# Attention heads of the second block in pairs on the two halves of TensorE's columns

## The chip, the cores and the metric

The kernel runs on one core of a Trainium2 chip. The metric is the device time of one execution in microseconds (us); of three runs the median was 3005.82 us. All data are 32-bit floats unless said otherwise.

## The reference

The reference is two transformer blocks on one sequence of 512 tokens and width 1024. The first block (a gated delta rule, a sliding-window attention and a mixture of 32 experts) is not touched. The second block adds a context of 256 tokens and has two layers. Only its attention matters here:

```
layer 1, latent heads (8) and grouped-query heads (8, two heads of keys and values):
    o  = softmax(q k^T * scale) v      for 512 queries over 768 keys (512 tokens + 256 context)
    oc = softmax(qc kc^T * scale) vc   for 256 context queries over the 256 context keys
    mix = concat(o of all heads) * silu(gate);   x = x + gate' * (mix @ w_out)
layer 2, windowed heads (8, two heads of keys and values):
    512 queries in blocks of 128, each over its own block, the one before, the one after (masked)
    and the 256 context keys, with a sink term per head in the softmax's sum
```

A head's values are 64 wide, its queries and keys 64 (grouped-query, windowed) or 96 (latent).

## The kernel before

Four stretches do this attention with the same three functions, one per engine (`pe_attention`, `dve_attention`, `act_attention`, lines 2268 to 2404): the grouped-query heads (`gqa`, 48 units), the latent heads 0 to 3 (`mla0`, 24), the latent heads 4 to 7 (`mla1`, 24) and, in the next layer, the windowed heads (`win`, 32). All engines meet (`meet()`) after each stretch.

A unit is one tile of 128 queries of one head. In layer 1 a head is two groups: one of four main units (768 keys) and one of two late units (the context's queries, 256 keys). In layer 2 a head is one group of four units of 512 or 640 keys. A unit goes through these steps:

- `score` (TensorE, line 2280): the query tile against the keys, into one of two PSUM buffers.
- `soften` (VectorE, line 2333 and after): the row maximum and its negative; in `win` masks are added before it (line 2324).
- `exponentials` (ScalarE, line 2381): the exponential with the row sum.
- `scale` (VectorE, lines 2349 and 2351): the reciprocal of the sum, and the row scaled by it.
- `turn_probs` (TensorE, line 222): each 128x128 tile of probabilities is transposed into a third PSUM buffer; `copy_probs` (ScalarE, line 2391) copies them to `PTM` (main), `PTC` (late) or `PTW` (windowed).
- `values` (TensorE, line 2299), once per group: for each of six key tiles (two for a late group), values (128 keys x 64) as the stationary operand, turned probabilities (128 keys x up to 512 queries) as the moving one, accumulated in PSUM bank 6 on partitions 0 to 63 for even heads, 64 to 127 for odd ones. Each such product shows as two records in the trace. VectorE then multiplies the 64 x 512 (or 64 x 256) result into the gate (line 2358).

The order on TensorE is written out: in iteration x come the scores of unit x+1, then the value products due (`A.sums[x]`), then the turning of unit x-1. `Heads` plans the due ones: when a group's last unit is x-1, its products are queued in iteration x, and from the next iteration on two are done in each. VectorE does maximum, scaling, and then the group's multiplication, in the iteration in which the group's last product is due, and waits there for it. `copy_probs` of a group waits until the values of the group two before are done.

In `gqa` and `mla0` further work for the latent heads (projections, norms, rotations, turnings) is advanced by a generator (`steps(filler, rate)`) twice (gqa) or four times (mla0) in each iteration on every engine.

Weights come through a ring. In the second block load n (2 MB or less) goes to slot n mod 3 and is issued by SP's queue, in order, when the load before it in its slot has been used. Loads 6 and 7 are the two halves of the output projection `w_out` of layer 1 (lines 1284 to 1296: the first half for all six row tiles, then the second), load 8 the first of layer 2. The arrays QT, KT, PTM and PTC lie in `spare`, behind the three slots.

## Time and profile before

| | us |
|---|---|
| median of three runs | 3005.82 (3004.95 to 3008.05) |
| the profiled execution | 3011.71 |
| its span | 3010.5 |
| TensorE busy | 2664.7 (89% of the span) |
| VectorE busy | 1008.3 (33%) |
| ScalarE busy | 565.4 (19%) |
| mean granted TensorE clock | 0.932 of 2.4 GHz |

The four stretches of attention lie at 2117.3 to 2548.6 us of the span (one after the other: gqa, mla0, mla1) and at 2834.5 to 2951.2 us (win). Busy time is the time in which an engine had at least one instruction running; the idle time of an engine that is not the one waited for costs nothing. "PEclk" is the granted clock as a share of 2.4 GHz: 0.50 is 1.2 GHz.

### The profile page before, as it was taken

What the parts mean: (1) busy time and instruction counts of PE and PEld (TensorE: products, weight loads), DVE (VectorE), ACT (ScalarE), POOL (GpSimd) and SP (SyncE); (2) the same over time, 40 slices, a digit from 0 to 9 for tenths busy, and PEclk for the clock granted to TensorE, in tenths of its full rate; (3) what the DMA queues carried; (4) which work ended last, traced back from release to release, by engine and by line L of the source; (5) the groups of instructions that cost most, each with busy time, mean ns of one, the idle gap of its engine ahead of it and who ended that gap; (6) DMA issues with size and microseconds to landing.
All of it is one profiled execution on the core that took longest, in us unless ns stands there. A gap on an engine that the chain in (4) does not pass through costs nothing. (4 is left out here: it accounts for less than half of the span.)

```text
span 3010.5 us, 27117 instructions
## 1 busy us (share of the span) xinstructions
PE 2664.7 (89%) x10307; PEld 1285.1 (43%) x10307; DVE 1008.3 (33%) x2147; ACT 565.4 (19%) x1272; POOL 170.3 (6%) x317
## 2 busy tenths in 40 slices
PE   6989879757999999999999997689898779999998
PEld 2544647343433433443433333355443334454443
DVE  2664444351111111211111111523455644332262
ACT  1354321100000000000000001111444443110250
POOL 0000422101000000000000001000000000000000
PEclk8989999868999999999999998799899899999899
DMA  8111195417999999769589996020000000022000
GB/s 310 60 56 43 53 366 214 168 42 271 403 414 415 406 415 417 314 246 391 189 358 414 419 416 255 28 81 28 28 1 1 1 28 22 14 84 84 28 1 28
DMA packets 143355, 565.43 MB, mean 188 GB/s; under 512 B 15429, under 2 KB 36158, under 8 KB 105202
## 3 DMA queue, kind: packets, MB, share of 16 engines
q1 hardware_dynamic: 127336, 515.97, 43.7%
q0 software_dynamic: 13136, 43.04, 3.8%
q10 hardware_dynamic: 2746, 4.61, 0.5%
q8 instruction: 85, 1.39, 0.2%
q14 instruction: 52, 0.43, 0.0%
HBM read 537.24 MB, written 26.35 MB: 187 GB/s over the span
## 5 line engine op out<-in xcount | busy, mean ns | idle before, releaser
L1585 PE MATMUL ps<-ring,mem 128*32 128x512 f32 (+2 forms) x1888 | 517.8, 601 | 11.8 <-issue 11.8
L216 PE MATMUL ps<-mem,ring 128*128 128x512 f32 (+1 forms) x1056 | 423.3, 561 | 2.6 <-DVE mem L736 1.6
L216 PE MATMUL ps<-ring,mem 128*128 128x512 f32 (+5 forms) x1136 | 392.8, 503 | 32.5 <-DVEq L181 15.0
L1585 PEld LDWEIGHTS ps<-ring,mem 128*32 128x32 f32 (+2 forms) x1888 | 189.6, 146 | 279.7 <-issue 279.7
L222 PE MATMUL ps<-mem 128*128 128x128 f32 (+3 forms) x1211 | 200.3, 301 | 113.1 <-DVE mem L1930 48.1
L216 PEld LDWEIGHTS ps<-mem,ring 128*128 128x128 f32 x1056 | 201.8, 192 | 214.0 <-issue 205.2
L216 PEld LDWEIGHTS ps<-ring,mem 128*128 128x128 f32 x1136 | 201.4, 196 | 209.9 <-issue 174.5
L1614 PE MATMUL ps<-ring,mem 128*32 128x512 f32 (+2 forms) x1056 | 271.0, 605 | 12.5 <-issue 12.5
L222 PEld LDWEIGHTS ps<-mem 128*128 128x128 f32 (+3 forms) x1211 | 150.6, 151 | 248.5 <-issue 153.3
L1585 PE MATMUL ps<-mem 128*32 128x512 f32 (+2 forms) x800 | 234.9, 596 | 1.7 <-issue 1.7
L1646 DVE COPY mem<-ps 128x512 f32<-128x512 f32 x48 | 33.3, 693 | 521.4 <-PE ps L222 521.4
L1654 ACT ACTIVATE mem<-mem 128x512 f32<-128x512 f32 x48 | 28.1, 632 | 784.7 <-DVE mem L1630 784.7
L1622 DVE COPY mem<-ps 128x512 f32<-128x512 f32 x48 | 33.3, 693 | 410.1 <-PE ps L222 410.1
L1614 PEld LDWEIGHTS ps<-ring,mem 128*32 128x32 f32 (+2 forms) x1056 | 99.8, 141 | 161.1 <-issue 161.1
L2280 PE MATMUL ps<-ring 64*128 64x256 f32 (+4 forms) x328 | 128.9, 514 | 27.7 <-ACT mem L2381 13.5
L1585 PEld LDWEIGHTS ps<-mem 128*32 128x32 f32 (+2 forms) x800 | 84.5, 145 | 107.7 <-issue 107.7
L2299 PE MATMUL ps<-ring,mem 128*64 128x512 f32 (+1 forms) x256 | 120.3, 597 | 5.4 <-ACT ring L2391 2.8
L2333 DVE TENSOR_REDUCE mem<-ps 128x1 f32<-128x768 f32 (+2 forms) x128 | 98.6, 770 | 71.0 <-PE ps L2280 66.4
L1614 PE MATMUL ps<-mem 128*128 128x512 f32 (+2 forms) x288 | 121.2, 601 | 0.0
L2057 ACT ACTIVATE mem<-ps 128x512 f32<-128x512 f32 (+2 forms) x68 | 33.2, 489 | 344.1 <-PE ps L216 337.1
L2280 PEld LDWEIGHTS ps<-ring 64*128 64x128 f32 (+1 forms) x328 | 60.3, 206 | 78.0 <-issue 46.3
L2381 ACT ACTIVATE mem<-ps,mem 128x768 f32<-128x768 f32 (+1 forms) x96 | 72.8, 759 | 87.9 <-DVE mem L2338 85.9
(363 smaller groups left out, 2387.2 us busy)
## 6 DMA issues: line engine op xcount, KB each, us to landing
ring<-in_w_up SPq DMA_DIRECT2D x91, 2048.0 KB, 16.1
ring<-in_w_down SPq DMA_DIRECT2D x47, 2048.0 KB, 22.8
mem<-in_w_up SPq DMA_DIRECT2D x37, 2048.0 KB, 18.8
mem<-in_w_down SPq DMA_DIRECT2D x17, 2048.0 KB, 20.3
ring<-in_w_ada SPq DMA_DIRECT2D x12, 2048.0 KB, 7.6
ring<-in_mod_w SPq DMA_DIRECT2D x8, 2048.0 KB, 10.3
y_rows<-mem POOLq DMA_DIRECT2D x24, 512.0 KB, 8.2
ring<-in_cd_w_in SPq DMA_DIRECT2D x6, 2048.0 KB, 7.8
```

The source lines that it names most:

```text
L216: i = e.matmul(o, l, r, start=(n == 0), stop=(n == len(pairs) - 1))
L222: r = e.transpose(o, i, ident[0:k, 0:k])
L1585: m = e.matmul(PS[n][c0:c0 + rows, :], XGT[:, u, k * 128 + c0:k * 128 + c0 + rows], wt[:, kk, n * 512:n * 512 + 512], start=False, stop=(k ...
L1614: m = e.matmul(PS[6 + n][c0:c0 + rows, :], ACTT[:, k * 128 + c0:k * 128 + c0 + rows], wt[:, kk, n * 512:n * 512 + 512], start=False, stop= ...
L1622: e.tensor_copy(XGT[:, i % 2, hh * 512:hh * 512 + 512], PS[4]).then_inc(L.x_copied, 1)
L1646: e.tensor_copy(ACTT[:, hh * 512:hh * 512 + 512], PS[5]).then_inc(L.a_copied, 1)
L1654: e.activation(SG[:, c], T1[:, c], ACT.Sigmoid, scale=1.702).then_inc(L.gate, 1)
L2057: e.activation(dst, bank[key][:, 0:n], func).then_inc(*empties(key))
L2280: m = e.matmul(PP[x % 2][:, at:at + k.shape[1]], q, k, start=True, stop=True)
L2299: m = e.matmul(PS[6][p0:p0 + 64, c0:c1], v, buf[:, k, c0:c1], start=(j == 0), stop=(j == len(vals) - 1))
L2333: e.tensor_reduce(m[:, 0:1], PP[x % 2][:, lo:lo + n], AX.X, ALU.max).then_inc(*dve.up())
L2381: e.activation(PB[:, x % 2, 0:n], PP[x % 2][:, lo:lo + n], ACT.Exp, bias=m[:, 0:1], accum_out=m[:, 1:2]).then_inc(*signal("exped").up())
```

## The change

The heads are taken in pairs. A group now holds the units of two heads: eight main ones (first the four of head a, then of head b), or four late ones, or eight windowed ones. Each unit carries the number `a` (0 or 1) of its head in the pair, and its turned probabilities go to the buffer of this number. A group's values are done in pairs: for each key tile first the product of head 0 to partitions 0 to 63 and right behind it that of head 1 to partitions 64 to 127. VectorE multiplies all 128 partitions in one instruction. `Heads` has a `rate`: two pairs of products in an iteration in layer 1, one in `win`.

The second buffers lie in ring slot 1 (layer 1), and in `spare` and slot 2 (`win`, four buffers). So SP's queue issues loads up to n_late = n_first + 7 only (n_first is the first load of the second block, so this one is "load 7"), and goes on after the last values of `mla1`.

```diff
--- before.py
+++ after.py
@@ -2236,13 +2236,17 @@
                 e.indirect_dma_start(YG[:, u, :], None, YD,
                                      bass.IndirectOffsetOnAxis(ap=DEST[:, n:n + 1], axis=0)).then_inc(*dyg[u].up(16))
 
-    QT, KT, PTM = R(0, 4, 768), R(3072, 2, 768), R(4608, 6, 512)
-    PTC = spare[:, 7680:8192].rearrange("p (k n) -> p k n", n=256)
+
+    QT, KT = R(0, 4, 768), R(3072, 2, 768)
+    PTM = [b[:, 0:3072].rearrange("p (k n) -> p k n", n=512) for b in (spare[:, 4608:], slot(1))]
+    PTC = [b[:, 3072:3584].rearrange("p (k n) -> p k n", n=256) for b in (spare[:, 4608:], slot(1))]
+    n_late = n_first + 7
+    assert slot_of(n_late) == 1
     pe_layer1(nc.tensor)
     dve_layer1(nc.vector)
     act_layer1(nc.scalar)
     pool_layer1(nc.gpsimd)
-    load_on(nc.sync, len(loads))
+    load_on(nc.sync, n_late)
     meet()
     next_stage()
 
@@ -2250,7 +2254,7 @@
     class Heads:
 
 
-        def __init__(self, tag, groups):
+        def __init__(self, tag, groups, rate):
             self.tag, self.groups, self.units = tag, groups, []
             for g, grp in enumerate(groups):
                 for n, u in enumerate(grp[0]):
@@ -2259,7 +2263,7 @@
             todo = []
             for x, u in enumerate(self.units):
 
-                self.sums[x], todo = todo[:2], todo[2:]
+                self.sums[x], todo = todo[:rate], todo[rate:]
                 if x and self.units[x - 1][1]:
                     todo += self.of(x - 1)
             self.sums["end"] = todo + self.of(len(self.units) - 1)
@@ -2290,13 +2294,15 @@
             done[A.tag, "turn", x] = pe.now()
 
         def values(sums):
+
             for g, j, x, k, v, c0, c1 in sums:
-                buf, vals, (p0, dst) = A.groups[g][1], A.groups[g][2], A.groups[g][4]
+                bufs, vals = A.groups[g][1], A.groups[g][2]
                 if j == 0:
                     e.wait_ge(*copied.at(x + 1))
                     if g:
                         e.wait_ge(*taken_.at(g))
-                m = e.matmul(PS[6][p0:p0 + 64, c0:c1], v, buf[:, k, c0:c1], start=(j == 0), stop=(j == len(vals) - 1))
+                for a in range(2):
+                    m = e.matmul(PS[6][64 * a:64 * a + 64, c0:c1], v[a], bufs[a][:, k, c0:c1], start=(j == 0), stop=(j == len(vals) - 1))
                 if j == len(vals) - 1:
                     m.then_inc(*pe.up())
                     done[A.tag, "values", g] = pe.now()
@@ -2353,9 +2359,9 @@
         def values(sums):
             for g, j, x, k, v, c0, c1 in sums:
                 if j == len(A.groups[g][2]) - 1:
-                    n, (p0, dst) = A.groups[g][3], A.groups[g][4]
+                    n, dst = A.groups[g][3], A.groups[g][4]
                     e.wait_ge(*done[A.tag, "values", g])
-                    e.tensor_tensor(dst, dst, PS[6][p0:p0 + 64, 0:n], ALU.mult).then_inc(*signal("values_taken").up())
+                    e.tensor_tensor(dst, dst, PS[6][:, 0:n], ALU.mult).then_inc(*signal("values_taken").up())
 
         masks(0)
         for x in range(len(units)):
@@ -2383,12 +2389,12 @@
                 e.activation(m[:, 2:3], m[:, 0:1], ACT.Exp, bias=sink).then_inc(*signal("sunk").up())
 
         def copy_probs(x):
-            g, end, c, places = units[x][0], units[x][1], units[x][8], units[x][9]
+            g, end, c, places, a = units[x][0], units[x][1], units[x][8], units[x][9], units[x][10]
             e.wait_ge(*done[A.tag, "turn", x])
             if g >= 2:
                 e.wait_ge(*done[A.tag, "values", g - 2])
             for k0, k1, to in places:
-                m = e.activation(A.groups[g][1][:, to:to + k1 - k0, c * 128:c * 128 + 128],
+                m = e.activation(A.groups[g][1][a][:, to:to + k1 - k0, c * 128:c * 128 + 128],
                                  PP[2][:, k0 * 128:k1 * 128].rearrange("p (k n) -> p k n", n=128), ACT.Copy)
             m.then_inc(*signal("probs_copied").up())
 
@@ -2408,16 +2414,17 @@
 
     def dense(H, qs, kts, vals, tile):
         groups = []
-        for h in range(H):
-            q, k, p0 = qs(h), kts(h), 64 * (h % 2)
-            units = [(q[:, i * 128:i * 128 + 128], [(k[:, 0:512], 0), (k[:, 512:768], 512)], 0, 768, [], None, i,
-                      [(0, 6, 0)]) for i in range(4)]
-            groups.append((units, PTM, [(j, vals(h, j), 0, 512) for j in range(6)], 512,
-                           (p0, GTE[p0:p0 + 64, tile + h // 2, 0:512])))
-            units = [(q[:, i * 128:i * 128 + 128], [(k[:, 512:768], 512)], 512, 256, [], None, i - 4, [(0, 2, 0)])
-                     for i in (4, 5)]
-            groups.append((units, PTC, [(j, vals(h, 4 + j), 0, 256) for j in range(2)], 256,
-                           (p0, GTE[p0:p0 + 64, tile + h // 2, 512:768])))
+        for m in range(H // 2):
+            main, late = [], []
+            for a in range(2):
+                q, k = qs(2 * m + a), kts(2 * m + a)
+                main += [(q[:, i * 128:i * 128 + 128], [(k[:, 0:512], 0), (k[:, 512:768], 512)], 0, 768, [], None, i,
+                          [(0, 6, 0)], a) for i in range(4)]
+                late += [(q[:, i * 128:i * 128 + 128], [(k[:, 512:768], 512)], 512, 256, [], None, i - 4, [(0, 2, 0)], a)
+                         for i in (4, 5)]
+            both = lambda j: (vals(2 * m, j), vals(2 * m + 1, j))
+            groups.append((main, PTM, [(j, both(j), 0, 512) for j in range(6)], 512, GTE[:, tile + m, 0:512]))
+            groups.append((late, PTC, [(j, both(4 + j), 0, 256) for j in range(2)], 256, GTE[:, tile + m, 512:768]))
         return groups
 
     gq_ = GQ.rearrange("p a n -> p (a n)")
@@ -2558,30 +2565,31 @@
                               KR[:, i, :].unsqueeze(1).to_broadcast([128, 4, 32])).then_inc(*signal("kr_copied").up())
 
     gqa = Heads("gqa", dense(8, lambda h: QT[half(h), h // 2, :], lambda h: KT[half(h), h // 4, :],
-                             lambda h, k: GKV[:, k, 128 + 64 * (h // 4):192 + 64 * (h // 4)], 4))
+                             lambda h, k: GKV[:, k, 128 + 64 * (h // 4):192 + 64 * (h // 4)], 4), 2)
     pe_attention(nc.tensor, gqa, PB, pe_latent(nc.tensor, 0), 1)
     dve_attention(nc.vector, gqa, PB, dve_latent(nc.vector, 0), 1)
     act_attention(nc.scalar, gqa, PB, act_latent(nc.scalar, 0), 1)
     pool_latent(nc.gpsimd, 0)
-    load_on(nc.sync, len(loads))
+    load_on(nc.sync, n_late)
     meet()
     next_stage()
 
     def mla(hh):
         return Heads(f"mla{hh}", dense(4, lambda h: LQ[hh][0:96, h, :], lambda h: LK[hh][h // 2][0:96, h % 2, :],
-                                       lambda h, k: LV[hh][:, k, h * 64:h * 64 + 64], hh * 2))
+                                       lambda h, k: LV[hh][:, k, h * 64:h * 64 + 64], hh * 2), 2)
 
     mla0, mla1 = mla(0), mla(1)
     pe_attention(nc.tensor, mla0, PB, pe_latent(nc.tensor, 1), 2)
     dve_attention(nc.vector, mla0, PB, dve_latent(nc.vector, 1), 2)
     act_attention(nc.scalar, mla0, PB, act_latent(nc.scalar, 1), 2)
     pool_latent(nc.gpsimd, 1)
-    load_on(nc.sync, len(loads))
+    load_on(nc.sync, n_late)
     meet()
     next_stage()
     pe_attention(nc.tensor, mla1, PB, no_filler(), 2)
     dve_attention(nc.vector, mla1, PB, no_filler(), 2)
     act_attention(nc.scalar, mla1, PB, no_filler(), 2)
+    nc.sync.wait_ge(*done["mla1", "values", len(mla1.groups) - 1])
     meet()
     next_stage()
 
@@ -2748,29 +2756,32 @@
     next_stage()
 
 
-    PTW = [HT.rearrange("p a n -> p (a n)")[:, a * 3072:a * 3072 + 3072].rearrange("p (k n) -> p k n", n=512) for a in range(2)]
+    assert slot_of(len(loads) - 3) == 2
+    ht = HT.rearrange("p a n -> p (a n)")
+    PTW = [b[:, 0:3072].rearrange("p (k n) -> p k n", n=512) for b in (ht, ht[:, 3072:], spare[:, 5120:], slot(2))]
     PB = R(3584, 2, 768)
     wmp, wmn = c3[:, 384:512], c3[:, 512:640]
 
     def windows():
         groups = []
-        for h in range(8):
-            q, k, p0 = QT[half(h), h // 2, :], KT[half(h), h // 4, :], 64 * (h % 2)
+        for m in range(4):
             units = []
-            for n in range(4):
+            for a, n in [(a, n) for a in range(2) for n in range(4)]:
+                q, k = QT[half(a), m, :], KT[half(a), m // 2, :]
                 lo, hi = max(n - 1, 0), min(n + 2, 4)
                 L = (hi - lo) * 128
                 at = 512 - L
                 masks = ([(wmp, at)] if n else []) + ([(wmn, 384)] if n < 3 else [])
-                units.append((q[:, n * 128:n * 128 + 128], [(k[:, lo * 128:hi * 128], at), (k[:, 512:768], 512)],
-                              at, L + 256, masks, sinkr[:, 8 + h:9 + h], n, [(0, hi - lo, lo), (hi - lo, hi - lo + 2, 4)]))
-            v = lambda j: PKV[:, j, 128 + 64 * (h // 4):192 + 64 * (h // 4)]
+                units.append((q[:, n * 128:n * 128 + 128], [(k[:, lo * 128:hi * 128], at), (k[:, 512:768], 512)], at, L + 256,
+                              masks, sinkr[:, 8 + 2 * m + a:9 + 2 * m + a], n, [(0, hi - lo, lo), (hi - lo, hi - lo + 2, 4)], a))
+            v = lambda j: (PKV[:, j, 128 + 64 * (m // 2):192 + 64 * (m // 2)],) * 2
             vals = [(j, v(j), 0, 512) for j in (4, 5)] \
                 + [(j, v(j), max(j - 1, 0) * 128, min(j + 2, 4) * 128) for j in range(4)]
-            groups.append((units, PTW[h % 2], vals, 512, (p0, MT[p0:p0 + 64, h // 2, :])))
+            bufs = PTW[0:2] if m % 2 == 0 else PTW[2:4]
+            groups.append((units, bufs, vals, 512, MT[:, m, :]))
         return groups
 
-    win = Heads("win", windows())
+    win = Heads("win", windows(), 1)
     pe_attention(nc.tensor, win, PB, no_filler(), 1)
     dve_attention(nc.vector, win, PB, no_filler(), 1)
     act_attention(nc.scalar, win, PB, no_filler(), 1)
```

## Rows read from the trace of the kernel before

**Rows 1.** Busy time by stretch: start:end, us, then per engine busy (count).

```profile
core 0: us, PE busy (x) PEld busy (x) DVE busy (x) ACT busy (x) POOL busy (x), PEclk, DMA share, GB/s
2117.30:2329.30 212.00, 188.35 (x608) 85.37 (x609) 119.03 (x310) 92.72 (x190) 2.15 (x6) 0.90 0.00 1
2329.30:2466.50 137.20, 109.26 (x352) 52.41 (x352) 76.21 (x206) 57.06 (x117) 1.70 (x6) 0.86 0.05 16
2466.50:2548.60 82.10, 70.59 (x256) 33.62 (x257) 41.70 (x105) 34.70 (x72) 0.00 (x0) 0.98 0.00 1
2834.50:2951.20 116.70, 104.30 (x368) 52.96 (x369) 73.02 (x216) 57.23 (x165) 0.00 (x0) 0.88 0.00 1
```

**Rows 2.** Groups of line 2299: xcount, then busy us, mean ns, and idle before.

```profile
L2299 PE MATMUL ps<-ring,mem 128*64 128x512 f32 (+1 forms) x256 | 120.3, 597 | 5.4 <-ACT ring L2391 2.8
...
L2299 PE MATMUL ps<-mem 128*64 128x512 f32 (+2 forms) x96 | 38.6, 530 | 0.7 <-ACT mem L2391 0.7
```

**Rows 3.** Chain of waits in mla1: start us, us, what.

```profile
2484.06 1.86 PE ps L2299 x4
...
2493.77 1.29 PE ps L2280 x4
...
2511.51 0.80 PE ps L222 x6
```

**Rows 4.** Timeline of VectorE, row maxima of mla1: start us, us, instruction.

```profile
2474.63 0.95 DVE L2333 TENSOR_REDUCE mem<-ps 128x1 f32<-128x768 f32 x1
...
2477.56 0.95 DVE L2333 TENSOR_REDUCE mem<-ps 128x1 f32<-128x768 f32 x1
...
2480.49 0.42 DVE L2333 TENSOR_REDUCE mem<-ps 128x1 f32<-128x256 f32 x1
...
2482.19 0.42 DVE L2333 TENSOR_REDUCE mem<-ps 128x1 f32<-128x256 f32 x1
...
2484.09 0.96 DVE L2333 TENSOR_REDUCE mem<-ps 128x1 f32<-128x768 f32 x1
...
2503.19 0.95 DVE L2333 TENSOR_REDUCE mem<-ps 128x1 f32<-128x768 f32 x1
```

**Rows 5.** Groups in the expert stage, 1164.2 to 1170.1 and 1007 to 1035.

```profile
L1585 PE MATMUL ps<-ring,mem 128*64 128x512 f32 x30 | 6.7, 594 | 3.4 <-issue 3.4
...
L1585 PE MATMUL ps<-ring,mem 128*128 128x512 f32 x63 | 27.8, 594 | 0.0
```

**Rows 6.** Timeline of VectorE, a multiplication of values and gate.

```profile
2493.00 0.68 DVE L2358 TENSOR_TENSOR mem<-mem,ps 64x512 f32<-64x512 f32 x1 [1.03 <-PE ps L2299]
```

**Rows 7.** Timeline of VectorE, first maxima of windowed heads 0 and 2.

```profile
2838.40 0.69 DVE L2333 TENSOR_REDUCE mem<-ps 128x1 f32<-128x512 f32 x1
...
2868.28 0.68 DVE L2333 TENSOR_REDUCE mem<-ps 128x1 f32<-128x512 f32 x1
```

**Rows 8.** Timeline of VectorE, maxima of mla0 around latent projections.

```profile
2331.07 0.96 DVE L2333 TENSOR_REDUCE mem<-ps 128x1 f32<-128x768 f32 x1 [1.91 <-PE ps L2280]
...
2342.56 0.96 DVE L2333 TENSOR_REDUCE mem<-ps 128x1 f32<-128x768 f32 x1
...
2366.63 0.95 DVE L2333 TENSOR_REDUCE mem<-ps 128x1 f32<-128x768 f32 x1
...
2382.86 0.96 DVE L2333 TENSOR_REDUCE mem<-ps 128x1 f32<-128x768 f32 x1
```

**Rows 9.** Timeline of mla0 at the lower clock, then busy time of two stretches.

```profile
2352.81 0.96 DVE L2333 TENSOR_REDUCE mem<-ps 128x1 f32<-128x768 f32 x1
...
2356.79 0.42 DVE L2333 TENSOR_REDUCE mem<-ps 128x1 f32<-128x256 f32 x1
...
2360.91 3.28 PE L2299 MATMUL ps<-ring,mem 128*64 128x512 f32 x4
...
2346.60:2363.70 17.10, 12.19 (x30) 6.56 (x30) 15.21 (x50) 6.86 (x13) 0.00 (x0) 0.50 0.00 1
...
2472.90:2476.30 3.40, 2.52 (x13) 1.45 (x11) 1.80 (x4) 2.16 (x4) 0.00 (x0) 1.00 0.00 0
```

**Rows 10.** DMA issues from 2020 us on: count, size, us from issue to landing.

```profile
ring<-in_ab_w_out SPq DMA_DIRECT2D x2, 2048.0 KB, 7.8
```

## The prediction

> **What bounds the kernel now.** I read the sums by stretch first. The second block's attention runs in four stretches: grouped-query heads (212 us), latent heads 0 to 3 (137 us) and 4 to 7 (82 us), windowed heads (117 us) [rows 1]. TensorE is busy 80 to 89% of each, VectorE 51 to 63%, ScalarE 42 to 49%: TensorE is the most loaded engine, but it has holes, so freed TensorE time isn't all won. Together 548 us; nothing outside them changes. The value products (line 2299) hold TensorE for 120.3 + 38.6 = 158.9 us, a figure that includes records at the lower clock [rows 2].
>
> Next the chain of waits and VectorE's timeline in the third stretch, which has no other work mixed in. A unit is one 128-row query tile of one head. Where a unit carries value products, the chain is TensorE throughout: score 1.29, two single value products (four records) 1.86, six turned tiles 0.80 us [rows 3]. Where it carries none, one row maximum follows the last after 2.93 us for a main unit (768 keys; 2474.63 to 2477.56) and 1.71 for a late one (256 keys; 2480.49 to 2482.19), whatever TensorE does: the loop maximum, exponential on ScalarE, reciprocal, scaling [rows 4]. One head of four main and two late units would be 4 x 2.93 + 2 x 1.70 = 15.1 us at that pace; it takes 19.1 (2484.09 to 2503.19) [rows 4]. So each head pays **4.0 us** for its values beyond the softmax loop.
>
> **Part 1: two heads on the array's halves.** Line 2299's instruction count stays; its order becomes head a, head b, head a, ... on output partitions 0-63 and 64-127. The trace has this form in the expert stage: 30 records of 128*64 over 512 columns take 6.7 us, 0.22 us each, against 27.8/63 = 0.44 us for records that use all columns [rows 5]. So a pair of value products costs what one costs now. TensorE work drops by half of 158.9, 79 us, at most; that is the outer end of the gain, the inner end is nothing (the softmax loop hides it).
>
> What is freed on the path, for a pair of heads in the third stretch: the pair is now 8 main units and then 4 late ones, and its six main pairs of products are due in late units 2 to 4, two pairs each, its two late pairs in the second unit of the next pair. I walk the four late units from the first one's maximum (t=0). The last main tile is copied at 1.9; pairs of products then take 1.9 to 3.75 and 4.4 to 6.2 between scores and turns, and 7.8 to 9.6 after the next main score (1.29). VectorE waits for these last ones and multiplies them into the gate (0.68, as the 64-row one now: it has the same columns [rows 6]). The next main maximum starts at 10.3 in place of the loop's 6.8: 3.5 us lost. The late pair costs one multiplication more, 0.4. Excess 4.0 us **per pair of heads**, where it was 4.0 per head. A stage's last head or pair ends in a tail that stays as long: now four main and two late single products stand behind the last unit, afterwards two pairs of late ones, but the main ones wait behind its late units: by the same walk it ends 0.1 us apart from now.
> - Latent heads, each of two stretches of 4: three full excesses before the last head become one before the last pair: 3 x 4.0 - 4.0, and the first head's four units have none in both: 8 us, and as the later heads' walk had 3.9 to 4.0 each and the pair's tail absorbs part, I keep 8 to 11 each, **10** taken.
> - Grouped-query, 8 heads: seven become three: **16**.
> - Windowed: the first two heads (29.9 us, 2838.40 to 2868.28 [rows 7]) run at half clock with value products in units 5 to 7; with none there, at the pace of 3.1 us a unit that the neighbours show, about 26. That is 4; each further pair loses one 0.68 multiplication [rows 6]: 2. **6**.
>
> Sum 42 at full clock.
>
> **Part 2: products mixed in.** In the first two stretches the latent projections (full-array products) are spread over units by index, and this index doesn't move. Where they met value products, the unit had TensorE full and paid for them wholly: 16.2 us (2366.63 to 2382.86) against 11.5 for the like unit without values (2331.07 to 2342.56) [rows 8]. Afterwards they fall largely into main units without values. Three such meetings at 3 to 5 us: **+10**, between 0 and 15.
>
> **Part 3: the clock.** The mean granted clocks 0.90, 0.86, 0.98 and 0.88 [rows 1] mean 2 x (0.10 x 212 + 0.14 x 137 + 0.02 x 82 + 0.12 x 117) = 112 us at 1.2 GHz. In 2346.6 to 2363.7, all at 0.50, TensorE was busy 12.2 of 17.1 us with scores and turns alone, until values came at 2360.9; 2.4 GHz followed them [rows 9]. At 1.2 GHz a main unit took 3.98 us (2352.81 to 2356.79) in place of 2.93, two value products 3.28 in place of 1.86 [rows 9, 3]. The change makes runs without values longer: seven or eight units of twelve in place of two of six. If a fall comes, it lasts until the next values: up to five main units, 5 x 1.05, and the first value products cold, 1.5 to 3: 8 us per fall. There are 8 such runs in the dense stretches. Against it, TensorE is 74% busy there (2.52 of 3.40 us in 2472.9 to 2476.3, where the clock held [rows 9]), and of the 112 us of now, which cost 26% of themselves by 2.93 against 3.98, 29 us, some 20 lie beside value products that move. I take four lasting falls, 32, less these 20, and a little more for values met cold: **-15**, between +15 and -65.
> The Trainium skill has a rule that speaks against this change: "TensorE: Matmul & The Clock Gate" (Part 1 and Part 4) says the default state is throttled, that activity releases it, and that transposes don't count as activity the same way. By it the long runs of scores and turns would all be cold; that is the rival below, and the trace agrees with it in 2346.6 to 2363.7 but not in 2472.9 to 2476.3 [rows 9].
>
> **Part 4: buffers and loads.** The turned probabilities of the second head lie in ring slot 1, so load 7 (second half of the output projection's weights, 2 MB) is issued only after the last latent values. It lands 7.8 us after issue [rows 10]; the projection uses the first half for 6 x 8 products of two records at 0.44, 42 us, before it waits for it. Cost nothing; without that cover 8 us. Loads behind it in SP's queue (8, the next layer's first) are needed after the whole projection, some 85 us. SP waits for the values alone, and no other work stands in its queue then. Buffers: a tile copy waits for the values of two groups back; they are done by late unit 4 and the next group's second unit, while the copy that wants them is a whole group later: no wait. The windowed heads get four buffers for two, no new wait. VectorE's final multiplications halve in number (40 to 20), counted above.
>
> **Sum.** 10 + 10 + 16 + 6 + 10 - 15 = 37 us. The profiled execution took 3011.71 us (3010.5 of span); it becomes 2974.7. The median shown is 3005.82, 5.9 us less, so the prediction is 3005.8 - 37, about **2969 us**.
>
> **Rivals.**
> - *The clock gives back more than the halves win.* Place: units without values; all 8 dense runs and the windowed start fall at once and stay down. About 58 main units (some 7 in 8 runs) x 1.05 = 61, plus 8 cold value starts x 3 = 24, less the 20 paid now: 65 lost against 52 won: +13, **3019 us**. It decides from about 50 cold units. For: 2346.6 to 2363.7. Against: 2472.9 to 2476.3, and the projection products keep the clock in four runs. Chance 0.05.
> - *The halves don't run at once*, so the change doesn't do what it says: four products of 0.86 in each late unit, 10.2 us excess per pair in place of 4.0 (five dense pairs stand before the last of their stretch: 31), three tails 5 us longer, the windowed one 4: 42 - 50 and the mixing gain lost: **3014 us**. Against: the expert records at 0.22 us. Chance 0.03.
> - *Softmax loop hides more*: VectorE's waits in the late units eat the mixing gain, falls cost 30: 42 - 30 = 12: **2994 us**. For: VectorE is 51 to 63% busy and waits in line for its own scalings [rows 1], and the walk leaves it 3.5 us idle per pair. Chance 0.2.
> - *TensorE is the bound throughout*: all of part 1's outer end at no clock loss, 65 to 79: **2935 us**. For: TensorE 89% busy in the first stretch. Chance 0.15.
> - My forecast: 0.57.
>
> Range 2940 to 2996. A measurement of this kernel tells 0.2%, 6 us, from no change. Slower 0.08 (the first two rivals), same 0.04 (an end of the third), faster 0.88.
>
> **What would show it.** Half as many final multiplications, on 128 partitions, of unchanged length. Busy time of line 2299's groups near half of 159 us. In the third stretch 12 units in about 34 us (38 before), the stretch near 71 us; TensorE idle in it grows. Clock of the four stretches: about 0.85 to 0.9 in the mean. Maxima 2.93 us apart in main units at 2.4 GHz, 3.98 at 1.2. First latent stretch 137 to about 122, first stretch 212 to about 195, windowed 117 to about 111. No wait of TensorE on load 7. Wrong if line 2299's busy time doesn't fall, if a main run sits at 0.50 in every pair, or if TensorE waits for a weight load at the output projection.

## The result, and the profile after

The changed kernel takes **2976.43 us** in the median of four runs (2972.64 to 2978.94), the kernel before 3006.94 in the same rounds: a ratio of 0.9897, 95% interval 0.988 to 0.9914, so 31 us or 1.0% faster. The forecast was 2969 us, in a range of 2940 to 2996. The profiled execution has a span of 2971.4 us, 39.1 shorter. (Spans differ by more than medians here: the profiled execution of before, 3011.71 us, lies above its other runs, that of after, 2972.64, is the fastest of its four.)

The busy times of the four stretches of attention, which answer to [rows 1] (start:end, us, then per engine busy and count; the edges are from the first score to the last multiplication):

```profile
2113.40:2307.40 194.00, 173.91 (x608) 84.30 (x608) 114.34 (x302) 91.98 (x190) 2.06 (x6) 0.82 0.00 1
2307.60:2429.00 121.40, 93.88 (x352) 48.95 (x352) 74.47 (x202) 56.46 (x117) 1.71 (x6) 0.89 0.00 1
2429.10:2502.30 73.20, 58.18 (x256) 30.36 (x256) 39.06 (x100) 34.36 (x72) 0.00 (x0) 0.98 0.00 1
2791.70:2912.00 120.30, 107.92 (x368) 56.02 (x368) 70.31 (x212) 55.20 (x161) 0.00 (x0) 0.70 0.00 1
```

With the same kind of edges the kernel before has 211.8, 137.5, 81.6 and 114.3 us (its rows with these edges are below):

```profile
2117.40:2329.20 211.80, 188.33 (x608) 85.30 (x608) 119.03 (x310) 92.72 (x190) 2.11 (x6) 0.90 0.00 1
2329.30:2466.80 137.50, 109.26 (x352) 52.41 (x352) 76.48 (x206) 57.06 (x117) 1.70 (x6) 0.86 0.05 16
2466.90:2548.50 81.60, 70.59 (x256) 33.59 (x256) 41.44 (x104) 34.70 (x72) 0.00 (x0) 0.98 0.00 1
2836.80:2951.10 114.30, 104.25 (x368) 52.89 (x368) 73.02 (x216) 55.31 (x161) 0.00 (x0) 0.88 0.00 1
```

The three dense stretches give 17.8 + 16.1 + 8.4 = 42.3 us. The windowed one **costs 6.0 us more** than before, at a mean granted clock of 0.70 in place of 0.88. That is 36.3 net; the stage between them is 1.1 us longer, and the first attention started 4.0 us earlier, which is in code that the change leaves alone. These stretches repeat far better than the whole: in the five kernels whose code for it is the same, the first one took 193.9 or 194.0 us each time, while the place where it began lay anywhere from 2111 to 2121 us. So the stretches are compared below beside the medians. The third stretch is less steady than that: 73.2 us in these five, but 75.4 in experiment 8, whose code for it is the same too and where the clock was at 1.2 GHz for 10.2 us of it in place of 3.4. (In the experiments' rounds the kernel before had medians of 3009.9 to 3010.6 us, some 3 to 4 above its rounds here; the ratios take that out.)

The groups of the value products, which answer to [rows 2] (count, then busy us, mean ns):

```profile
L2305 PE MATMUL ps<-ring,mem 128*64 128x512 f32 (+2 forms) x304 | 78.6, 644 | 4.2 <-ACT ring L2397 4.2
...
L2305 PE MATMUL ps<-mem 128*64 128x512 f32 (+2 forms) x48 | 13.1, 628 | 0.0
```

The same 352 records hold TensorE for 91.7 us in place of 158.9. In the chain of waits of the third stretch one sees why: eight records where [rows 3] had four, in the same time.

```profile
2459.13 1.87 PE ps L2305 x8
2461.00 0.37 PE ps L222 x2
2461.37 1.29 PE ps L2284 x4
2462.66 1.89 PE ps L2305 x8
```

VectorE's timeline around them (first late maximum, last late one, the wait for the values, the next main maximum, and the first late maximum of the next pair), for [rows 4] and [rows 6]:

```profile
2454.43 0.42 DVE L2339 TENSOR_REDUCE mem<-ps 128x1 f32<-128x256 f32 x1
...
2460.08 0.42 DVE L2339 TENSOR_REDUCE mem<-ps 128x1 f32<-128x256 f32 x1
...
2464.58 0.69 DVE L2364 TENSOR_TENSOR mem<-mem,ps 128x512 f32<-128x512 f32 x1 [1.74 <-PE ps L2305]
2465.18 0.95 DVE L2339 TENSOR_REDUCE mem<-ps 128x1 f32<-128x768 f32 x1
...
2488.96 0.42 DVE L2339 TENSOR_REDUCE mem<-ps 128x1 f32<-128x256 f32 x1
```

Twelve units take 2488.96 - 2454.43 = 34.5 us, where two heads took 2 x 19. The load that was put off: SP issues it as soon as the last values are done, it lands 13.8 us later (7.8 in [rows 10]), and TensorE goes on with the output projection, 57.5 us busy of 57.6.

```profile
2501.90 0.37 SPq L401 DMA_DIRECT2D ring<-in_ab_w_out  x1
...
2502.40:2560.00 57.60, 57.52 (x140) 26.01 (x141) 12.30 (x20) 3.50 (x5) 0.00 (x0) 1.00 0.34 119
```

### The profile page after: what moved, and what is told of

It is laid out like the page before. It is cut to its first block and busy times, and to the rows that moved or that the text cites. A ratio compares the mean times of both kernels' runs of the same rounds, so it can differ in the third digit from the quotient of the medians.

```text
span 2971.4 us, 27052 instructions
## 1 busy us (share of the span) xinstructions
PE 2630.7 (89%) x10307; PEld 1281.3 (43%) x10307; DVE 996.9 (34%) x2127; ACT 563.7 (19%) x1272; POOL 170.1 (6%) x317
## 5 line engine op out<-in xcount | busy, mean ns | idle before, releaser
L1614 PE MATMUL ps<-ring,mem 128*32 128x512 f32 (+2 forms) x1056 | 271.3, 609 | 10.2 <-issue 10.2
L2284 PE MATMUL ps<-ring 64*128 64x256 f32 (+4 forms) x328 | 146.4, 573 | 32.1 <-ACT mem L2387 18.1
L2339 DVE TENSOR_REDUCE mem<-ps 128x1 f32<-128x768 f32 (+3 forms) x128 | 98.5, 770 | 70.9 <-PE ps L2284 66.3
L2284 PEld LDWEIGHTS ps<-ring 64*128 64x128 f32 (+1 forms) x328 | 67.6, 231 | 89.2 <-issue 52.7
L2397 ACT ACTIVATE ring<-ps 128x768 f32<-128x768 f32 (+2 forms) x128 | 75.2, 600 | 91.2 <-PE ps L222 90.8
## 6 DMA issues: line engine op xcount, KB each, us to landing
ring<-in_mod_w SPq DMA_DIRECT2D x8, 2048.0 KB, 10.2
```

Of the source, the lines that this page charges most:

```text
L1614: m = e.matmul(PS[6 + n][c0:c0 + rows, :], ACTT[:, k * 128 + c0:k * 128 + c0 + rows], wt[:, kk, n * 512:n * 512 + 512], start=False, stop= ...
L2284: m = e.matmul(PP[x % 2][:, at:at + k.shape[1]], q, k, start=True, stop=True)
L2339: e.tensor_reduce(m[:, 0:1], PP[x % 2][:, lo:lo + n], AX.X, ALU.max).then_inc(*dve.up())
L2397: m = e.activation(A.groups[g][1][a][:, to:to + k1 - k0, c * 128:c * 128 + 128], PP[2][:, k0 * 128:k1 * 128].rearrange("p (k n) -> p k n", ...
```

## The experiments

**1. Windowed heads alone back to single ones.**

```diff
-        for m in range(4):                                   # pairs
+        for h in range(8):                                   # one head, p0 = 64 * (h % 2)
...
-            groups.append((units, bufs, vals, 512, MT[:, m, :]))
+            groups.append((units, [PTW[a]], vals, 512, MT[64 * a:64 * a + 64, m, :], (64 * a,)))
...
-    win = Heads("win", windows(), 1)
+    win = Heads("win", windows(), 2)
```

> Only the windowed heads go back to one head at a time (two single value products an iteration, 64 partitions); layer 1 keeps the pairs. In the profiles the windowed stretch took 114.3 us before and 120.3 us after the change, with 27 and 72 us of it at 1.2 GHz. Theory (the pair form suits the dense heads and loses in the windowed ones, because its iterations hold too little array work to keep 2.4 GHz): stretch about 114 us, time 2976 - 6 = 2970 us. Rival (the 6 us are an accident of when the clock fell in one execution): time 2976 us, stretch 114 to 120 at will.

Median 2968.34 us, ratio 0.9856 (0.9839 to 0.9873); the changed kernel has 0.9897. The windowed stretch is back at the length and the clock of before (27 us at 1.2 GHz):

```profile
2799.40:2913.40 114.00, 104.14 (x368) 52.84 (x368) 72.95 (x216) 55.27 (x161) 0.00 (x0) 0.88 0.00 1
```

The loss belongs to the pair form there, and it is no accident of one execution: the interval lies wholly under that of the changed kernel (0.988 to 0.9914).

**2. All of head a, then all of head b.**

```diff
-            for g, j, x, k, v, c0, c1 in sums:
...
-                for a in range(2):
-                    m = e.matmul(...)
+                for a in range(2):
+                    for g, j, x, k, v, c0, c1 in part:       # part: the products of this iteration
+                        m = e.matmul(...)
```

> Same pairs, buffers, waits and count of instructions; only the order of the value products inside an iteration differs: all due products of head a, then all of head b, so that neighbours in the queue use the same half of the columns. Theory (the gain is that neighbours on different halves run at once): busy time of the value products in the three dense stretches from 65 back towards 120 us, dense stretches 20 to 35 us longer, time 3000 to 3012 us. Rival (the gain comes from fewer waits of VectorE and the regrouping, half as many final multiplications): under 8 us longer, 2976 to 2984 us.

Median 2976.95 us, ratio 0.9888 (0.9872 to 0.9904), the dense stretches 194.0, 121.5 and 73.2 us. The rival's number (2976 to 2984 us) came true, but not by its reason: the trace says that the experiment didn't do what it was made for. TensorE's timeline in the third stretch (start us, us):

```profile
2461.61 1.95 PE L2306 MATMUL ps<-ring,mem 128*64 128x512 f32 x8
```

Eight records in 1.95 us again. The single records start in twos 0.01 to 0.02 us apart (2461.61 and 2461.62, 2462.09 and 2462.11, and so on). The trace doesn't name the half of a record, but neighbours on one half stood 0.46 us apart (four in 1.86 us, [rows 3]), so two that start together are on different halves: head b's products, four records behind in the queue, start with head a's. The theory was wrong in taking the order for the switch; what running at once is worth stays to be tested, in experiment 3. Only the tail of the windowed stretch changed (123.0 us in place of 120.3): there twelve records of head a stand before twelve of head b, and the 24 take 9.04 us in place of 6.21 (more on them in the last section).

**3. Full-width work between the two halves.**

```diff
-            values(A.sums[x])
+            values(A.sums[x], (0,))
             if x:
                 turn_probs(x - 1)
+            values(A.sums[x], (1,))
```

> Pairs as in the changed kernel, but in each iteration TensorE does head a's due value products, then the turning of the unit before (128 columns wide), then head b's due products, so that full-width work stands between the two halves. The order alone (all of a, then all of b) had kept the two halves running at once. Theory (running at once is the gain): in the third stretch the busy time of the value products goes from 14.5 back to 27 us, the stretch from 73 to 78 to 82 us; dense stretches together 15 to 30 us longer, time 2992 to 3010 us. Rival (regrouping and halved multiplications give the gain, and freed TensorE time is hidden anyway): busy time rises but the time stays under 2984 us.

Median 3027.94 us, ratio 1.0061 (1.0048 to 1.0074): the whole gain is gone and more. The dense stretches take 435.5 us together (changed kernel 388.6, before 430.8). The third stretch, its 512-column value products (48 records), and the value products of all four stretches:

```profile
2463.70:2549.90 86.20, 72.08 (x256) 34.55 (x256) 39.37 (x100) 34.23 (x72) 0.00 (x0) 0.94 0.00 1
...
L2306 PE MATMUL ps<-ring,mem 128*64 128x512 f32 x48 | 23.8, 663 | 0.0
...
L2306 PE MATMUL ps<-ring,mem 128*64 128x512 f32 (+2 forms) x304 | 132.6, 595 | 4.4 <-ACT ring L2399 4.3
...
L2306 PE MATMUL ps<-mem 128*64 128x512 f32 (+2 forms) x48 | 22.7, 556 | 0.0
```

The 48-record group in the changed kernel:

```profile
L2305 PE MATMUL ps<-ring,mem 128*64 128x512 f32 x48 | 12.4, 638 | 0.0
```

Running at once is what halves the busy time: without it all value products hold TensorE for 155.3 us, as before the change (158.9). The 3028 us are more than the expectation, which had taken part of the added busy time for hidden. In the third stretch TensorE is busy 13.9 us longer (72.1 against 58.2) and the stretch is 13.0 longer, so TensorE's idle time didn't grow (14.1 against 15.0). The edit also lets head b's products stand behind the turning and its waits (for the scaling and the copy), and VectorE behind both: one pair of row maxima stands 10.28 us apart in place of 5.11. How much of the slowdown is this and how much the lost overlap was not separated; the doubling of the busy time doesn't depend on it.

**4. VectorE's multiplication in two instructions.**

```diff
-                    e.tensor_tensor(dst, dst, PS[6][:, 0:n], ALU.mult).then_inc(...)
+                    e.tensor_tensor(dst[0:64], dst[0:64], PS[6][0:64, 0:n], ALU.mult)
+                    e.tensor_tensor(dst[64:128], dst[64:128], PS[6][64:128, 0:n], ALU.mult).then_inc(...)
```

> As the changed kernel, but VectorE multiplies each pair's result in two instructions of 64 partitions, as many as before the change (40 in place of 20). Theory (the halved multiplications are a small term, one more wait-free instruction per group): each added one stands in the softmax loop with 0.62 us (512 columns) or 0.35 (256): 12 x 0.6 + 8 x 0.35 = 10 us if all are on the path, 5 to 10 us longer, time 2981 to 2986. Rival (VectorE has slack there): under 2 us.

Median 2990.87 us, ratio 0.9939 (0.9923 to 0.9954). By stretch 2.8 + 3.6 + 3.7 + 1.0 = 11 us longer:

```profile
2115.40:2312.20 196.80, 173.98 (x608) 85.50 (x608) 119.22 (x310) 92.26 (x190) 1.71 (x6) 0.83 0.00 1
2312.30:2437.30 125.00, 96.16 (x352) 50.32 (x352) 76.93 (x206) 56.60 (x117) 1.71 (x6) 0.86 0.00 1
2437.50:2514.40 76.90, 59.85 (x256) 30.44 (x256) 41.56 (x104) 34.25 (x72) 0.00 (x0) 0.96 0.00 1
2803.90:2925.20 121.30, 105.77 (x368) 55.23 (x368) 73.46 (x216) 55.19 (x161) 0.00 (x0) 0.72 0.00 1
```

So up to 10 of the 42 us won in the dense stretches aren't TensorE's at all: one instruction on 128 partitions does what two on 64 did, in the 0.68 us of one of them, and VectorE has no slack there. It is up to 10, as the clock fell a little more too: time at 1.2 GHz is 109 us in the dense stretches in place of 99. In the third, one late unit takes 3.81 us in place of 2.23 where the clock was low (2464.2 to 2467.6), which leaves about 2 of its 3.7 us to the instructions.

**5. Two pairs an iteration in the windows.**

```diff
-    win = Heads("win", windows(), 1)
+    win = Heads("win", windows(), 2)
```

> Windowed heads in pairs with two pairs of products an iteration in place of one: three iterations with values and five without, for one head pair. Theory (clock): denser bursts lift the clock sooner, but the run without products is longer (five of eight in place of two); stretch 116 to 122 us, time within 4 us of 2976. Rival (the windowed loss comes from one pair per iteration making the last products late, waits of VectorE): stretch 112 us or less, time 2968 us.

Median 2974.11 us, ratio 0.9887 (0.9868 to 0.9906); the stretch 120.8 us at a clock of 0.69. As the clock theory had it (75 us at 1.2 GHz, 72 in the changed kernel); how the products are grouped doesn't matter here.

**6. A product of constant data in the windowed iterations that have no values.** The output of the product is read by nobody.

```diff
+            if A.tag == "win" and not A.sums[x]:
+                e.matmul(PS[7], X[:, 0, 0:128], X[:, 0, 0:512], start=True, stop=True)
```

> Windowed heads in pairs as in the changed kernel, and in each windowed iteration that has no value products (the first nine, then two of eight) TensorE does one more product of 128x128 on 512 columns of constant data into an unused bank, 0.86 us at 2.4 GHz; nobody reads it. Theory (the clock makes the windowed loss): the clock rises within the first units and stays; stretch from 120 to about 104 us although TensorE has about 15 products more, time about 2961 us. Rival (waits of the pair form make it): stretch 120 us or longer by up to 13 us, time 2976 to 2990 us.

Median 2966.22 us, ratio 0.9861 (0.9841 to 0.9881). More work on TensorE (396 records in place of 368), and the stretch is 9.6 us shorter:

```profile
2789.90:2900.60 110.70, 98.27 (x396) 49.87 (x396) 69.58 (x212) 53.68 (x161) 0.00 (x0) 0.92 0.00 1
...
2791.50:2805.20 13.70, 13.52 (x27) 6.27 (x26) 7.57 (x22) 4.98 (x13) 0.00 (x0) 0.50 0.00 1
2805.20:2893.90 88.70, 77.66 (x341) 40.40 (x341) 61.06 (x188) 48.24 (x148) 0.00 (x0) 1.00 0.00 1
```

The clock rises after 13.7 us and stays up for 88.7 (it falls once more, for 3.4 us, at the end); without the product the changed kernel began with 41 us at 1.2 GHz and fell three times more:

```profile
2793.30:2834.30 41.00, 38.83 (x97) 21.07 (x96) 24.49 (x74) 18.93 (x53) 0.00 (x0) 0.50 0.00 1
...
2793.30:2825.90 32.60, 30.43 (x77) 17.38 (x75) 20.28 (x61) 17.01 (x47) 0.00 (x0) 0.50 0.00 1
...
2847.90:2861.60 13.70, 13.50 (x32) 6.25 (x33) 8.09 (x25) 5.29 (x18) 0.00 (x0) 0.50 0.00 1
```

The first value product of the changed kernel starts at 2825.9 us. Up to there TensorE was busy 30.4 of 32.6 us: at 1.2 GHz it is nearly full with scores (64 rows) and turns (128 rows) and stays at 1.2 GHz all the same. The three later falls (2847.9, 2875.2 and 2902.5 us) come after the last values of a pair of heads, in the units that have none. The stretch missed the 104 us of the expectation, since the softmax loop takes over: 2.8 to 3.1 us a unit at either amount of TensorE work.

**7. The same, single heads in the windows.**

```diff
     (the windows of experiment 1)
+            if A.tag == "win" and x < 4:
+                e.matmul(PS[7], X[:, 0, 0:128], X[:, 0, 0:512], start=True, stop=True)
```

> Layer 1 in pairs, windowed heads one at a time as before the change, with the additional product of constant data (128x128 on 512 columns) in the first four windowed iterations only. Theory (the cold start is what the windowed stretch loses in both forms): cold time 27 to about 14 us, stretch 114.0 to 109 or 110 us, as the pairs with it (110.8); time 2964 us. Rival (the pairs are worth their halved work once the clock is high): stretch 112 us or more.

Median 2968.64 us, ratio 0.9863 (0.9848 to 0.9877); the stretch 113.7 us at 0.91. Here the rival was right: with the clock up on both sides the pairs are 3.0 us ahead (110.7 against 113.7), and the cold start alone was worth almost nothing to the single form (114.0 to 113.7, time at 1.2 GHz 27 to 20 us): while the clock is low the added products are on the path themselves, units 2 and 3 taking 4.3 and 4.5 us in place of 3.1 and 2.8.

**8. Products of constant data in the dense stretches too.**

```diff
+            if A.tag in ("gqa", "mla0") and x >= 3 and x % 12 in range(2, 9):
+                if x >= 12:
+                    e.wait_ge(*taken_.at(x // 12 * 2))
+                e.matmul(PS[6][:, 0:384], X[:, 0, 0:128], X[:, 0, 0:384], start=True, stop=True)
```

> Pairs, with the additional product of constant data in the windowed iterations without values, and now also in the grouped-query and first latent stretch: 128x128 on 384 columns, 0.65 us, into bank 6 between two groups, in six or seven iterations of twelve. Nobody reads it. Theory (units without values at 1.2 GHz are what the pairs lose): cold time of the first stretch from 68 to under 25 us, stretch from 194 to 182 to 188 us, second from 121 to 117; time 2950 to 2958 us. Rival (TensorE's added 20 us are on the path, since latent projections fill the same iterations, or the cold units were hidden behind VectorE's latent work): stretch 194 us or longer, time 2966 us or more.

Median 2956.84 us, ratio 0.9837 (0.9821 to 0.9853).

```profile
2113.20:2299.10 185.90, 170.31 (x662) 85.22 (x662) 114.24 (x302) 92.74 (x190) 2.06 (x6) 0.94 0.00 1
2299.30:2420.50 121.20, 97.32 (x378) 52.52 (x378) 74.33 (x202) 56.90 (x117) 1.70 (x6) 0.92 0.00 1
```

The first stretch gains 8.1 us (clock 0.82 to 0.94, time at 1.2 GHz 68 to 20 us, as the theory had it), the second nothing (0.2, where 4 were expected): its clock hardly changed (0.89 to 0.92). The third, which got no such products, is 2.2 us longer (75.4): its clock fell more, 10.2 us in place of 3.4.

**9. The kernel before with such products**, in two of six iterations and in the first four of the windows.

```diff
+            if A.tag == "win" and x < 4:
+                e.matmul(PS[7], X[:, 0, 0:128], X[:, 0, 0:512], start=True, stop=True)
+            if A.tag in ("gqa", "mla0") and x >= 3 and x % 6 in (3, 4):
+                if x >= 6:
+                    e.wait_ge(*taken_.at(x // 6 * 2))
+                e.matmul(PS[6][:, 0:384], X[:, 0, 0:128], X[:, 0, 0:384], start=True, stop=True)
```

> The kernel before the change (single heads) with the product of constant data that nobody reads in iterations without value products: in the grouped-query and first latent stretch two of six iterations (384 columns), in the windowed stretch the first four (512). Theory (the clock costs both kernels, the pairs more, since their runs without values are longer): the gain here is smaller than the 20 us that the pairs got from it (2976 to 2957): first stretch 212 to 203 or 206, second 137 to 135, windowed 114 to 111; time 2990 to 2998 against 3007. Rival (the single form gains as much, so the pairs' net gain stays 30 us at a high clock): 2987 or less.

Median 2994.97 us, ratio 0.9943 (0.9926 to 0.9959): the single form gains 0.6%, the pairs gained from 0.9897 to 0.9837, too. In the first stretch it goes from 211.8 to 201.1 us, more than the pairs did (8.1). Clock up on both sides, the pairs are 201.1 - 185.9 = 15.2, 135.3 - 121.2 = 14.1 and 113.7 - 110.8 = 2.9 us ahead:

```profile
2116.30:2317.40 201.10, 187.22 (x640) 87.62 (x640) 118.93 (x310) 93.38 (x190) 2.15 (x6) 0.96 0.00 1
2317.50:2452.80 135.30, 110.74 (x368) 54.95 (x368) 76.43 (x206) 57.35 (x117) 1.70 (x6) 0.90 0.05 16
```

So the median lies in the theory's range (2990 to 2998), but its reason fails: the single form gets more back in the first stretch than the pairs do, and only in the windows is it shown that the clock takes more from the pairs. Two things keep this from being exact. The pairs were given more added products (27 against 16 in the first stretch, 13 against 8 in the second), which hold TensorE themselves, and in the second stretch neither clock rose much (0.86 to 0.90, 0.89 to 0.92).

**10. The multiplication one iteration later.**

```diff
             scale(x)
-            values(A.sums[x])
+            if x:
+                values(A.sums[x - 1])
```

> The changed kernel, with VectorE's multiplication of a group's values moved one iteration later, so that it doesn't stand in the softmax loop waiting for the last pair of products. Theory (this wait is what is left of the excess: 5.1 to 5.3 us in the unit after a late one in place of 2.9): 2.0 us per main group of 8 dense pairs, less what TensorE holds anyway: third stretch 73 to 70 or 71 us, time 2976 - 8 to 14 = 2962 to 2968. Rival (TensorE is the bound in those units, the wait only shows it): under 3 us.

Median 2968.25 us, ratio 0.9864 (0.9843 to 0.9885), against 0.9897, so 8 us by the medians, at the lower end of the expectation (8 to 14): by stretch 3.4 and 2.7 us shorter, nothing in the third (73.3, where 70 or 71 was expected) and the fourth (120.5). In the third the clock hides what is won: it was low for 6.8 us in place of 3.4, and in experiment 11, where it never fell there, the third stretch takes 71.5. The wait moved: the row maxima around it stand 2.7 and 4.8 us apart where they stood 5.1 and 2.9. Together that is 7.5 us in place of 8.0: of the 2 us that VectorE waited here only 0.5 are won, the rest is TensorE's own work, as it seems.

**11. Both together, the fastest version.** The later multiplication and the products of constant data (dense: x % 12 from 3 to 8).

> The later multiplication together with the products of constant data that keep the clock (dense: five or six of twelve iterations; windowed: those without values). If both gains are separate terms: 2957 - 8 to 14 = 2943 to 2949 us, below every kernel so far. Rival (TensorE bound, or the constant products now wait for the later multiplication): 2955 us or more.

Median **2951.85 us**, ratio 0.9805 (0.9786 to 0.9824): below all others, and between the expectation (2943 to 2949) and its rival (2955 or more). By the ratios the two terms are separate (0.9897 - 0.0060 - 0.0033 = 0.9804); by the stretches they fall 2 us short of it.

```profile
2110.70:2295.90 185.20, 168.63 (x656) 84.58 (x656) 113.86 (x302) 93.01 (x190) 2.00 (x6) 0.94 0.00 1
2296.10:2419.50 123.40, 96.70 (x376) 52.73 (x376) 74.34 (x202) 56.83 (x117) 1.70 (x6) 0.92 0.00 1
2419.60:2491.10 71.50, 56.90 (x256) 29.92 (x256) 39.01 (x100) 34.22 (x72) 0.00 (x0) 1.00 0.00 1
2779.20:2888.80 109.60, 97.91 (x396) 49.70 (x396) 69.51 (x212) 53.59 (x161) 0.00 (x0) 0.92 0.00 1
```

The second stretch is 2.2 us longer than in experiment 8 and 4.7 longer than in experiment 10; why was not tried.

## Why the prediction was right, and where not

- **The halves run at once.** Right: 91.7 us busy for 158.9, and experiment 3 takes it away. The strict alternation that the change writes out isn't what does it: with four records of each head in an iteration the order doesn't matter (experiment 2).
- **The walk of the late units.** It gave 10.3 us from the first late maximum to the next main one and about 34 for twelve units; measured 10.75 and 34.5. Third stretch: 10 us forecast (8 by the walk's own sum), 8.4 measured, and not as the walk has it: from the first row maximum to the last it is 5.4 us shorter (70.3 to 64.9), and the tail behind the last maximum, which the walk had within 0.1 us of now, is 3.0 shorter (9.5 to 6.5). The last pair's values come within its late units too, and one of these units met 1.2 GHz (3.43 us in place of 2.23).
- **First and second stretch.** 195 and 122 us were written down for the profile; it shows 194.0 and 121.4. The terms behind them were 16 and 10, plus 10 for projections met by values, less most of 15 for the clock. The sum of the three dense stretches, 42.3, is above the 31 that 10 + 10 + 16 + 10 - 15 gives and below the 46 without the clock's term. No run tells the 10 for the projections apart from the rest.
- **The clock in the dense stretches.** The third part charged it with -15 in all. Time at 1.2 GHz rose by 14 us in the three stretches (85 to 99: 44 to 68 in the first, 38 to 27 in the second), which by the forecast's own price of 26% is 4 us lost. By experiments 8 and 9 the single form got 10.7 us back in the first stretch and the pairs 8.1 (2.2 and 0.2 in the second), which as a difference is 3 to 5 us won, though with unequal numbers of added products. So the sign stays open, but the term is small, not -15. The long runs of scores and turns weren't all cold, as they would be by the rule of the Trainium skill that the prediction cites ("TensorE: Matmul & The Clock Gate"): in the third stretch both runs of main units without value products kept their 2.93 us from maximum to maximum, and the clock was low for 3.4 us of 73.2.
- **The windowed stretch.** This is the step that failed, by its sign: "at the pace of 3.1 us a unit that the neighbours show", 6 us won. The walk took the windows' cold start as given and of fixed length. In the trace before it ended 24 us in, after the single heads' value products had begun in iteration 5; in pairs they start in iteration 9, it lasts 41 us, and the clock falls three times more in the units between two pairs' values, which it did once before: 72 us at 1.2 GHz in place of 27, and 6 us lost in place of 6 won. The rival "the clock gives back more than the halves win" was true of this one stretch and of no other. Experiments 1, 6 and 7 show it; with the clock up the pairs win 3.0 us here. The rule of the Trainium skill cited in the prediction ("TensorE: Matmul & The Clock Gate") bears on this stretch, and here the trace agrees with it: added products brought the clock back after 13.7 us, and 30.4 us of 32.6 busy with scores and turns did not (which of the two doesn't count, no run tells).
- **The multiplications.** Halved and of unchanged length, 0.68 us; their worth was within the walk, and experiment 4 puts it at up to 11 us, 10 of them dense.
- **Loads and buffers.** No wait of TensorE on the load put off (it took 13.8 us to land in place of 7.8, against some 42 of cover), none for buffers.
- **The other rivals.** "TensorE is the bound throughout" would have given the whole of the freed time: the value products freed 67 us and 36 came of it. "The softmax loop hides more" gave 2994 us, 18 above the measurement.

The errors, +11 in the dense stretches and -12 in the windows, nearly cancel, and that is luck: the total came within 8 us of the forecast, better than its parts.

## What to carry to other kernels

Where TensorE's products use half of the columns, work from two independent outputs, one on each half of the partitions, takes the time of one (here eight records in 1.87 us where four took 1.86), as long as no full-width instruction stands between them (experiment 3); the engine that empties them gets half as many instructions as well. Then look at what the freed stretches do to the granted clock: a phase that was kept at 2.4 GHz by the products that are now halved or moved may drop to 1.2 and give the gain back, and an idle-time product of constant data tells in one run whether it does. Read the gain per stretch, since the sum of two wrong terms can look right.

## What the runs showed of the hardware

- Value products on the second half of the columns start beside those of the first half even if they stand behind them in program order. At the end of experiment 2's windowed stretch twelve records of head a stand before twelve of head b, and the widths tell them apart, since each head's begin with four of 512 columns. Eight of a ran alone (the first six of them started at 1.2 GHz); b's first started 0.01 us after a's ninth (2912.36 us), and both ran side by side until a was done; then b ran alone.

```profile
2907.40:2912.35 4.95, 4.95 (x8) 1.72 (x9) 0.00 (x0) 0.00 (x0) 0.00 (x0) 0.57 0.00 0
2912.35:2913.60 1.25, 1.25 (x8) 0.74 (x7) 0.00 (x0) 0.00 (x0) 0.00 (x0) 1.00 0.00 0
2913.60:2916.45 2.85, 2.85 (x10) 1.10 (x8) 0.00 (x0) 0.00 (x0) 0.00 (x0) 1.00 0.00 0
```

  So the second half started when four records of the first were left, here as in the dense stretches (four before four), and not earlier. The Trainium skill ("TensorE: Matmul & The Clock Gate", Part 3) says that matmuls start and end in program order; b's first started before a's tenth in this trace, and the measurement decides.
- Added work can shorten a stretch: 28 more records in the windows, 9.6 us less, with the time at 1.2 GHz down from 72 to 17 us.
- A multiplication of 128 partitions and one of 64 take the same 0.68 us.
